# Three edits at the head of an encoder-block kernel: raw q and k tiles are copied before the next high half, ropes run before the low half, tile 1's high half comes in two pieces

## The reference, cut to what matters

```
n = RMSNorm(x)
[qA|kA|vA|qB|kB|vB|gA|gB] = n @ W_in
qA, kA: 4 heads x 2 x 64 channels each; of each 64 the first 16 are rotated:
    rot = concat([x1*cos - x2*sin, x2*cos + x1*sin]); the other 48 pass unchanged
qA = rope(qA) * 64**-0.5 ; kA = rope(kA)
p  = softmax(qA @ kA.T) ; a = p[0] - lam * p[1] ; yA = rmsnorm(a @ vA)
... neighbourhood attention, gated merge, W_out, residual,
... product-key retrieval of 16 experts per head out of 16384, final RMSNorm
```

## Time and profile before

| what | us |
|---|---|
| median of 3 runs | 1013.02 |
| lowest and highest | 1012.43, 1013.66 |
| the profiled execution, device time | 1012.58 |
| its span, first to last instruction | 1010.7 |
| TensorE busy in it | 1000.9 (99%) |
| VectorE busy | 839.9 (83%) |
| ScalarE busy | 604.9 (60%) |

### The profile page before, as it was taken

The page is one execution under the profiler, slowest core; times in us unless marked ns, Lnnn a source line. Parts: engine busy times, 40 slices in busy tenths (PEclk is TensorE's granted clock), DMA queues, the critical chain, the costliest instruction groups (busy, mean ns, idle before and its releaser), DMA issues.

```text
span 1010.7 us, 20524 instructions
## 1 busy us (share of the span) xinstructions
PE 1000.9 (99%) x6945; PEld 921.6 (91%) x6945; DVE 839.9 (83%) x1674; ACT 604.9 (60%) x1144; POOL 81.0 (8%) x38
## 2 busy tenths in 40 slices
PE   8999999999999999999999999999999999999997
PEld 8889999999999999999999999978888888888886
DVE  7888869769998989999999999777777777777776
ACT  6456544655545468888888888544444444444444
POOL 0000000277860000000000000000000000000000
PEclk9999999999999999999999999999999999999999
DMA  8744445645677766666666666887777777777772
GB/s 296 232 141 147 126 138 175 230 161 200 197 235 231 236 208 213 208 209 208 198 216 208 202 206 212 274 311 236 235 236 233 235 234 234 233 235 235 234 232 73
DMA packets 87749, 214.93 MB, mean 213 GB/s; under 512 B 9728, under 2 KB 43008, under 8 KB 87296
## 3 DMA queue, kind: packets, MB, share of 16 engines
q1 hardware_dynamic: 87104, 213.07, 65.3%
q10 hardware_dynamic: 576, 0.93, 0.3%
HBM read 195.08 MB, written 18.87 MB: 212 GB/s over the span
## 4 chain that ended last, share of the span: by engine, by line
PE 97%; DVE 1%; DMA 1%; issue 0%; ACT 0%; ACTq 0%
PE pO L1156 36%; PE pO L1441 18%; PE pTT L1473 17%; PE pM L1473 17%; PE pSS L1415 1%; PE pTT L1415 1%; DMA raw<-in_stream 1%; PE pSS L1221 1%; PE pSS L1379 1%; PE pM L1258 1%; PE pTT L1240 0%; PE pTT L1484 0%; PE pM L1252 0%; PE pTT L1233 0%; DVE wlos L699 0%
## 5 line engine op out<-in xcount | busy, mean ns | idle before, releaser
L475 ACT ACTIVATE whis<-raw 128x1024 fp32r<-128x1024 f32 x327 | 345.5, 1057 | 203.3 <-PE pM L1473 172.8
L1064 DVE TENSOR_TENSOR wlos<-raw,whis 128x1024 fp32r<-128x1024 f32 x125 | 153.3, 1226 | 87.5 <-ACT whis L475 87.4
L699 DVE TENSOR_TENSOR wlos<-raw,whis 128x1024 fp32r<-128x1024 f32 x169 | 205.1, 1219 | 14.7 <-ACT whis L475 14.2
L1156 PE MATMUL pO<-xhi,whis 128*128 128x256 f32 x752 | 212.2, 282 | 0.8 <-ACT qkT L519 0.8
L1156 PE MATMUL pO<-xlo,whis 128*128 128x256 f32 x752 | 210.0, 279 | 0.0
L1156 PE MATMUL pO<-xhi,wlos 128*128 128x256 f32 x752 | 209.8, 279 | 0.0
L1441 PE MATMUL pO<-xlo,whis 128*128 128x256 f32 x512 | 143.4, 280 | 0.0
L1156 PEld LDWEIGHTS pO<-xhi,whis 128*128 128x128 f32 x752 | 141.2, 188 | 2.2 <-issue 1.8
L1441 PE MATMUL pO<-xhi,wlos 128*128 128x256 f32 x512 | 143.0, 279 | 0.0
L1441 PE MATMUL pO<-xhi,whis 128*128 128x256 f32 x512 | 143.0, 279 | 0.0
L1156 PEld LDWEIGHTS pO<-xlo,whis 128*128 128x128 f32 x752 | 141.3, 188 | 0.0
(11 more groups left out here) (251 smaller groups left out, 1867.1 us busy)
## 6 DMA issues: line engine op xcount, KB each, us to landing
raw<-in_stream SPq DMA_DIRECT2D x199, 512.0 KB, 3.7
raw<-in_vrows SPq DMA_DIRECT2D x128, 512.0 KB, 3.5
a_scratch<-ast SPq DMA_DIRECT2D x128, 128.0 KB, 1.9
aring<-a_scratch SPq DMA_DIRECT2D x128, 128.0 KB, 3.3
biasm<-in_bias SPq DMA_DIRECT2D x8, 256.0 KB, 5.4
keysT<-in_keys SPq DMA_DIRECT2D x1, 1024.0 KB, 6.2
h_scratch<-h1tok SPq DMA_DIRECT2D x1, 1024.0 KB, 6.5
htok<-h_scratch SPq DMA_DIRECT2D x1, 1024.0 KB, 9.8
```

The costliest lines, as they stand in the source:

```text
L475: act.activation(whi[s], raw[s][:], ACT.Copy).then_inc(hi_ready, 1)
L699: dve.tensor_tensor(wlo[t % RING], raw[t % RING][:], whi[t % RING].bitcast(F32), ALU.subtract).then_inc(lo_ready, 1)
L1064: dve.tensor_tensor(wlo[s], raw[s][:], whi[s].bitcast(F32), ALU.subtract).then_inc(lo_ready, 1)
L1156: last = pe.matmul(dst, st, mv, start=(c == 0 and q == 0), stop=(c == len(terms) - 1 and q == 2))
```

## The change

The copy of a raw q or k tile out of PSUM, which came after the high half of tile k+3, now stands ahead of it; the copy of tile 0 stands even ahead of the squares and of tile 3's high half. The copy takes over the factor 1/8 of the queries, so that one pair of tables serves both halves and the second pair is not built. `rope` stands ahead of `low_front` in its step. Tile 1's high half is made in two pieces of 512 columns with a semaphore each, and in `two_tiles` the leftover products of tile 0 come one step earlier.

```diff
-            hi_at(1)
+            def raw_copy(k):
+
+                act.wait_ge(tile_done, k + 1)
+                act.activation(qkT[:, k, :], pO[k % 2][:, 0:T], ACT.Copy, scale=SCALE if k < HA else 1.0).then_inc(evac_act, 1)
+
+            for half in range(2):
+                part = slice(half * HALF, (half + 1) * HALF)
+                act.wait_ge(raw_landed[1], 16)
+                act.activation(whi[1][:, part], raw[1][:, part], ACT.Copy).then_inc(hi_ready if half else second_hi, 1)
             hi_at(2)
+            raw_copy(0)
             act.activation(gates[:, 0:C // 2, :], xT[:, 0:C // 2, :], ACT.Square).then_inc(squares, 1)
             hi_at(3)
             for k in range(T_PROJ):
+                if 0 < k < T_VA:
+                    raw_copy(k)
                 if k:
                     hi_at(k + LEAD)
                 if k < T_VA:
-
-                    act.wait_ge(tile_done, k + 1)
-                    act.activation(qkT[:, k, :], pO[k % 2][:, 0:T], ACT.Copy).then_inc(evac_act, 1)
                     if k == 3:
                         rms_root(1)
...
                 if part == 0:
-                    scale = 1.0 if half else SCALE
-                    link(dve.scalar_tensor_tensor(tables[:, 0, :], K("cos"), scale, rstd[:], ALU.mult, ALU.mult))
-                    link(dve.scalar_tensor_tensor(tables[:, 1, :], K("sin"), scale, rstd[:], ALU.mult, ALU.mult))
+                    if half == 0:
+                        dve.tensor_tensor(tables[:, 0, :], K("cos"), rstd[:], ALU.mult)
+                        link(dve.tensor_tensor(tables[:, 1, :], K("sin"), rstd[:], ALU.mult))
...
             for k in range(T_PROJ + 1):
+                if k in ROPE_AT:
+                    rope(*ROPE_AT[k])
                 if 0 < k < T_QB:
                     low_front(k + LEAD)
...
                 if k == 5:
                     lambda_rest()
-                if k in ROPE_AT:
-                    rope(*ROPE_AT[k])
...
                     high(0, c)
                     low(0, c)
-                    if c >= C - 2:
-                        rest(0, c - (C - 2))
-                for c in range(2, C - 2):
+                    if c > HALF:
+                        rest(0, c - HALF - 1)
+                for c in range(C - HALF - 1, C - 2):
                     rest(0, c)
-                pe.wait_ge(hi_ready, 1)
                 for c in range(C):
+                    if c == 0:
+                        pe.wait_ge(second_hi, 1)
+                    elif c == HALF:
+                        pe.wait_ge(hi_ready, 1)
                     high(1, c)
```

More of the change, by code:

```diff
@@ L272, in build @@
         head_landed = sem("head_landed")
+        second_hi = sem("second_hi")
         head_hi = sem("head_hi")
```

## The result

The changed kernel takes 1016.94 us (median of 7 executions, 1015.85 to 1017.29) against 1013.02 (7 executions, 1012.43 to 1013.68): ratio 1.0036 (the quotient of the two medians alone is 1.0039), 95% interval 1.0026 to 1.0045. It is 3.9 slower. The profiled execution took 1016.99, its span 1015.2, which is 4.5 more than before.

A forecast was written before the change was run, and what follows sets the result against it. TensorE, busy 1000.9 of 1010.7, was taken as the bound. Data +1.66 (3.18 - 1.52) plus clock 1.3 gave +3.0: 1016.0 against the median, 1015.6 on the profiled execution; own range 1014.9 to 1017.4, 8-in-10 range 1013.9 to 1017.6.

The forecast's parts named there:

- The true releaser of tile 8's wait: TensorE before tile 8, kernel before: start at 32.21 follows VectorE's tile 9 low half, ending 32.06, by 0.15.
- Tile 2 near 12.5, tile 3 at 16.06: TensorE's early tiles: earlier copies start tile 2 near 12.5, not 13.69, and tile 3 at 16.06, not 16.83; gain 0.77.
- ScalarE's detour of 0.82: Early copies of tiles 3 and 4 delay high halves on ScalarE; tile 7's low half starts 25.26 instead of 24.44.
- Tile 9's low half at 35.24, tile 8 at 35.39, silence 4.4: Ropes moved ahead end VectorE's low half 3.18 later, at 35.24; TensorE idles from 30.99 to 35.39.
- The scores no longer wait: First scores follow tile 12 directly because the second rope finishes in time: 46.00 instead of 47.52, a gain of 1.52.
- the sum: Start of first scores and end, without the clock: 3.18 - 1.52 = +1.66, with bounds +0.9 and +2.2.
- The fall of the clock: The 4.4 silence drops TensorE's clock for some 3.0 at 0.44 lost per microsecond: +1.3, taken as 0.7 to 2.2.
- rival 2: Clock stays low 5 or more, or falls late in a busy stretch: +1.66 + 2.2 or more, 1017 and above; chance 0.07.
- the main one: Long wait before tile 8 with a fall of the clock: +3.0, 1016.0 against the median; chance 0.60.
- the forecast's own range: End time from 1.66 - 0.5 + 0.7 to 2.2 + 2.2: 1014.9 to 1017.4.
- Rival 1: The long wait before tile 8 comes, but the clock stays up: +1.66, 1014.7; chance 0.25.
- Rival 3: Tile 8 finds its data, tile 9's low half ending before 30.8: up to 2.7 faster, 1010.3; chance 0.05 with partial forms.

The follow-up runs named there:

- the kernel with the filled silence: The changed kernel with 19 float32 matmuls of ones, read by nobody, in TensorE's wait before tile 8: 1014.80, ratio 1.0019.
- the version with late ropes: The changed kernel with ropes in later steps (7, 9, 10) and early copies only for tiles 0 to 2: 1009.66, ratio 0.9968 against the kernel before.
- the filled kernel: The changed kernel with ropes back behind their step's low half, plus 8 float32 matmuls of ones before tile 8's wait: 1012.75, ratio 0.9999.
- the kernel with the ropes back: The changed kernel with ropes put back behind the low half of their step, other edits kept: 1013.58, ratio 1.0008 against the kernel before.

## Why the prediction was right, point by point

- *The true releaser of tile 8's wait.* The argument that the wait in the row of tile 8 is for tile 9's low half on VectorE, though the row names ScalarE, carried the forecast. Right: moved behind the rope, that low half took tile 8 with it, and the row of after names it.
- *Tile 2 near 12.5, tile 3 at 16.06.* 12.65 and 16.00. Tile 2 did not wait for its low half, as I had it, but followed tile 1 without a wait; this changed nothing, since tile 3 waited for its own. The gain of 0.77 (0.83) was there and was swallowed by the later wait, as forecast. The two pieces bought nothing.
- *ScalarE's detour of 0.82.* Tile 6's low half at 20.50 (20.40 forecast), the norm at 21.64 (21.59), tile 7's low half at 25.35 (25.26). With the copies late again it is 24.54: the detour is 0.81.
- *Tile 9's low half at 35.24, tile 8 at 35.39, silence 4.4.* 35.40, 35.54 and 4.48.
- *The scores no longer wait.* Right. Without a fall of the clock they start at 49.37, +1.85 where the sum had +1.66. The difference is the 0.19 by which tile 8 starts later there than in the sum, 35.58 against 35.39.
- *The fall of the clock.* Right that it falls, and right in what a microsecond at the lower level costs: 0.44 by the sum, 2.56 in 5.54 = 0.46 in the profile. Two things in the term were weaker than they read. The rows of the start from which it was sized give a granted clock of 1.00 in both stretches, so the lower level there was inferred from the pace (7 matmuls in one stretch, 11 in the next) and not read; the changed kernel's row from 36 to 37, with 7 matmuls at a granted 0.50, bears it out. And the duration was mis-sized: I had taken the 3.0 for which the slow pace held after the first matmul at the start; here the lower level held for 5.5 after tile 8's start, while in two other profiles it was 3.4 in all. So the profiled execution lost 2.56 where the term had 1.3 and its upper end 2.2.
- *Which branch came.* By the prediction's own words the profiled execution, with 5.5 at the lower level, 2.56 for it and 1016.99 in all, is that of rival 2 ("5 or more", "1017 and above", chance 0.07), and not the main one. Five of the seven executions have its mean granted clock of 0.996 for the whole span; the two fastest, 1015.85 and 1016.01, have 0.997 and 0.998. In the medians the clock costs 1.85 to 2.14, inside the ends but near the upper one, and the data part 2.07: with 0.55 and 0.41 over my terms, 1.85 and 2.07 make the 0.9 by which the median came above the forecast. The direction and the path are earned; that the median, 1016.94, still lies inside the forecast's own range, whose upper end of 1017.4 was meant for at most 5 at the lower level, owes something to luck. The low end of the range was also not what its terms give: it used 1.66 - 0.5, where the sum's own bound was +0.9.
- *The page.* The sentence that I quoted from the Trainium skill (page "TensorE: Matmul & The Clock Gate", section "What's actually happening"), that activity releases the throttle, agrees with the kernels with a filled silence: matmuls whose results nobody reads kept the clock at 1.00.
- *Carried to the end.* The scores are 4.41 late, the span is 4.5 longer.

Rival 1 (clock stays up) is what the kernel with the filled silence shows: 1014.80 where it had 1014.7. Rival 3 (faster, if tile 9's low half is in time) would have given 1010.3, and the version with late ropes, which makes it so, has 1009.66.

## What to carry to other kernels

On an engine that works through its program in order, as VectorE and ScalarE do in every timeline here, moving a block of work ahead of an item delays that item by the whole block; look up who waits for it, and how much slack it had, before looking at what the block gains. Put such a block where its engine idles, and check the items around it one by one against the moments at which the busiest engine needs them. And a wait on TensorE like those here, from 2.1 to 4.5, can cost up to 2.6 beyond its own length, since the matmuls after it run at the lower clock.

## What the runs showed that I had not expected

A silence of 2.1 can already be enough: by the filled kernel it made the clock fall in about half of the executions of one kernel, and so gave that kernel two groups of times, 2 us apart.

The time from the last matmul to the fall is no fixed delay either. My prediction read 2.1 from the one fall that it had. In the kernels here it goes from 2.0 to 4.1: 2.0 at the end of the kernel with the ropes back, 3.2 in the wait of the changed kernel, 3.4 with only the ropes moved, and 4.1 in the changed kernel after its own end (its last matmul ends at 1009.72). With the copies late from tile 3 on, the fall came 4.1 after the last matmul before the silence, when TensorE had been at work again for 0.5. The rows of TensorE's windows, first the changed kernel, then the one with the late copies:

```profile
1009.00:1010.00 1.00, 0.72 (x7) 1.00 0.74 277
1010.00:1013.80 3.80, 0.00 (x0) 1.00 0.47 175
1013.90:1015.00 1.10, 0.00 (x0) 0.50 0.16 61
```

```profile
31.20:34.70 3.50, 0.00 (x0) 1.00 0.62 225
34.80:35.20 0.40, 0.40 (x4) 1.00 0.00 0
35.30:38.60 3.30, 3.30 (x18) 0.50 0.94 253
```

So the silence of 4.4 was not as clearly beyond the limit as my "2.1" made it look, and a single profile shows one case of several. The time at the lower level was 3.4 in the profiles with 3.31 and 3.61 of silence and 6.8 in the one with 4.48; one profile of each does not show whether the longer silence or the moment of the fall made the difference.

And 38 matmul passes of ones that compute nothing won 1.85 to 2.14 in the median by keeping TensorE busy during a wait.
